# Two layered blocks on one core: the last norms moved behind their projections, modulation sums by transposes, and one projection reordered

## The reference, cut to what matters

```python
for layer in range(2):                         # first block
    shift, scale, gate = split(silu(c) @ ada_w[layer, 0] + ada_b[layer, 0])
    h = rms_norm(x, norm_w[layer, 0]) * (1.0 + scale) + shift
    y = hybrid_attention_mixer(h) if layer == 0 else multiscale_pool_mixer(h)
    x = x + gate * y
    shift, scale, gate = split(silu(c) @ ada_w[layer, 1] + ada_b[layer, 1])
    h = rms_norm(x, norm_w[layer, 1]) * (1.0 + scale) + shift
    x = x + gate * (square(relu(h @ w1[layer])) @ w2[layer])
x = rms_norm(x, final_norm_w)
# second block
x = x + concat(moba_attention, retention)(rmsnorm(x, attn_norm)) @ w_out
h = rmsnorm(x, ffn_norm)
u = causal_dwconv(h @ w_up, conv_w, conv_b)    # 3 taps along the tokens, each feature by itself
x = x + (gelu(u) * (h @ w_gate)) @ w_down      # inner width 2816
g = sigmoid(rmsnorm(x, ple_norm) @ w_ple_gate)
x = x + (p @ w_ple) * g
return rmsnorm(x, final_norm)
```

## Time and profile before

| | |
|---|---|
| median of 3 runs | 1028.75 us (1027.26 to 1029.9) |
| the profiled execution: its own time | 1026.28 us |
| its span | 1024.6 us |
| TensorE busy | 933.2 us, 91% |
| VectorE, ScalarE, GpSimd busy | 690.8, 446.6, 56.4 us |
| chain that ended last | TensorE 74%, VectorE 15%, waits for nothing shown 5%, ScalarE 4% |

### The profile page before, as it was taken

How to read it: one execution, slowest core, us unless ns; L and a number is a source line. 1 busy time by engine, 2 the same in 40 slices (tenths; PEclk the granted TensorE clock), 3 DMA queues, 4 the chain that set the end, 5 groups by cost and what they waited for, 6 DMA issues and landing times.

```text
span 1024.6 us, 17857 instructions
## 1 busy us (share of the span) xinstructions
PE 933.2 (91%) x7128; PEld 892.6 (87%) x7128; DVE 690.8 (67%) x877; ACT 446.6 (44%) x532; POOL 56.4 (6%) x102
## 2 busy tenths in 40 slices
PE   1599988999999999889999999999887999999976
PEld 1398865989999999779999999888787999999976
DVE  4757887678887777766655555865547776766457
ACT  2225533236664333356563334544533545443352
POOL 2101111021111000000000000000000000000000
PEclk9779975889999999699999999999998999999989
DMA  9829664439998787137665453734413655545511
GB/s 319 301 83 357 224 220 151 165 116 305 319 332 295 272 272 255 41 111 238 209 240 166 164 195 133 227 124 137 151 52 113 191 178 183 196 156 186 194 42 42
DMA packets 156457, 196.09 MB, mean 191 GB/s; under 512 B 5325, under 2 KB 143100, under 8 KB 156412
## 3 DMA queue, kind: packets, MB, share of 16 engines
q1 hardware_dynamic: 142588, 145.12, 44.0%
q0 software_dynamic: 13824, 50.34, 13.3%
HBM read 194.38 MB, written 1.06 MB: 191 GB/s over the span
## 4 chain that ended last, share of the span: by engine, by line
PE 74%; DVE 15%; issue 5%; ACT 4%; DMA 1%; SPq 1%; DVEq 0%; ACTq 0%; POOLq 0%
PE G L527 15%; PE G L528 14%; PE G L529 14%; PE A L527 7%; PE A L529 7%; PE A L528 7%; DVE w_lo L985 3%; ACT w_hi L1599 2%; PE A L631 1%; PE A L611 1%; DVE ada_acc L1003 1%; PE G L585 1%; DVE HN L1134 1%; PE G L587 1%; PE G L586 1%
## 5 line engine op out<-in xcount | busy, mean ns | idle before, releaser
L985 DVE TENSOR_TENSOR w_lo<-raw,w_hi 128x2048 fp32r<-128x2048 f32 (+1 forms) x135 | 307.2, 2275 | 217.3 <-ACT w_hi L1599 217.1
L527 PE MATMUL G<-h_hi,w_hi 128*128 128x256 f32 x1288 | 379.2, 294 | 29.3 <-DVE h_lo L1114 13.3
L1599 ACT ACTIVATE w_hi<-raw 128x2048 fp32r<-128x2048 f32 (+1 forms) x135 | 256.6, 1901 | 327.6 <-PE G L529 173.6
L528 PE MATMUL G<-h_lo,w_hi 128*128 128x256 f32 x1288 | 373.5, 290 | 0.0
L529 PE MATMUL G<-h_hi,w_lo 128*128 128x256 f32 x1288 | 372.9, 290 | 0.0
L527 PEld LDWEIGHTS G<-h_hi,w_hi 128*128 128x128 f32 x1288 | 256.3, 199 | 36.4 <-issue 24.5
L528 PEld LDWEIGHTS G<-h_lo,w_hi 128*128 128x128 f32 x1288 | 256.9, 199 | 0.8 <-issue 0.8
L529 PEld LDWEIGHTS G<-h_hi,w_lo 128*128 128x128 f32 x1288 | 256.6, 199 | 0.0
L527 PE MATMUL A<-u_hi,w_hi 128*128 128x256 f32 x512 | 144.2, 282 | 1.1 <-DVE X L1094 0.8
L528 PE MATMUL A<-u_lo,w_hi 128*128 128x256 f32 x512 | 143.5, 280 | 0.0
L529 PE MATMUL A<-u_hi,w_lo 128*128 128x256 f32 x512 | 143.5, 280 | 0.0
(11 more groups left out here) (279 smaller groups left out, 1092.8 us busy)
## 6 DMA issues: line engine op xcount, KB each, us to landing
raw<-in_mlp_w_dram SPq DMA_DIRECT2D x64, 1024.0 KB, 5.5
ada_raw<-in_ada_w_dram POOLq DMA_DIRECT2D x90, 512.0 KB, 5.3
raw<-in_w_in_dram SPq DMA_DIRECT2D x14, 1024.0 KB, 5.0
raw<-in_w_up_dram SPq DMA_DIRECT2D x11, 1024.0 KB, 5.2
raw<-in_w_gate_dram SPq DMA_DIRECT2D x11, 1024.0 KB, 5.3
raw<-in_attn_w_in_dram SPq DMA_DIRECT2D x9, 1024.0 KB, 12.1
raw<-in_w_down_dram SPq DMA_DIRECT2D x8, 1024.0 KB, 5.2
raw<-in_attn_w_out_dram SPq DMA_DIRECT2D x4, 1024.0 KB, 7.1
```

Of the source, the lines that this page charges most:

```text
L527: pe.matmul(dst, wh, ah, start=start, stop=False)
L528: pe.matmul(dst, wh, al, start=False, stop=False)
L985: dve.tensor_tensor(w_lo[n % 2][:, 0:k, :], raw[n % RAW][:, 0:k, :], w_hi[n % 2][:, 0:k, :].bitcast(F32), ALU.subtract).then_inc(lo_done, 1)
L1599: act.activation(w_hi[n % 2][:, 0:k, :], raw[n % RAW][:, 0:k, :], ACT.Copy).then_inc(hi_done, 1)
```

## The change

It has four parts.

- **Feed-forward and last gate on X times the norm weight.** While the second output projection runs, ScalarE and VectorE make `e_hi` and `e_lo` = X * weight after each residual, without rstd. Block 96 is an `early_block` with the mean square inside, and the other feed-forward blocks (`gated_block`) read `e_hi`, `e_lo`. `gated_up` on VectorE multiplies the bank by rstd into `UP`, in place of ScalarE's copy; the gate block is left without rstd, and `residual_tile` multiplies the down projection by it. The last gate's `h_hi`, `h_lo` are X * weight, made tile pair by tile pair in the down projection; its mean square comes after the second group of block 130; VectorE multiplies each gate bank by rstd into `HN`, and ScalarE takes the sigmoid of that.
- **Modulation sums by transposes** for layers 0, 1 and 3 (`turn_sums`, `part`): four transposes into a bank, two banks per part, and VectorE adds along the rows. Layer 2 keeps single-column matmuls (`add_sums`), a bank for each part.
- **First output projection**: each residual comes ahead of the next weights' rest and the `ada` steps; the last squares are made by ScalarE, and the mean square adds two sources, so it has four matmuls.
- **Order**: scale of layer 2, then its mean square, then shift (read by VectorE after the second `pad` tile) and gate; the sums of layer 3 come after the pooling block.

```diff
-                  ("flip1", 3), ("flip2", 0), ("flip3", 1), ("ms0", 2), ("mod0", 3), ("glr", 2))
+                  ("flip1", 3), ("flip2", 0), ("flip3", 1), ("ms0", 2), ("scale0a", 3), ("scale0b", 0), ("shift0a", 1),
+                  ("shift0b", 2), ("glr", 2))
...
-        take_each(("go0", 0), ("go1", 1), ("gm0", 2), ("gm1", 3), ("mod1", 3), ("ms1", 2), ("gate1", 3),
-                  ("mod2", 3), ("ms2", 2), ("gate2", 0), ("mod3", 1), ("gate3", 3), ("ms3", 2), ("ms4", 2), ("ms5", 3))
+        take_each(("go0", 0), ("go1", 1), ("gm0", 2), ("gm1", 3),
+                  ("scale1a", 3), ("scale1b", 0), ("shift1a", 1), ("shift1b", 3), ("ms1", 2), ("gate1a", 0),
+                  ("gate1b", 1), ("scale2", 3), ("ms2", 2), ("shift2", 3), ("gate2", 0), ("scale3a", 3),
+                  ("scale3b", 2), ("shift3a", 0), ("shift3b", 1), ("ms3", 3), ("gate3a", 2), ("gate3b", 3),
+                  ("ms4", 2), ("ms5", 3))
...
+            def turn_sums(m, name, blocks):
+
+                part = PARTS.index(name)
+                for half in range(2):
+                    dst = bank_empty(pe, f"{name}{m}{'ab'[half]}")
                     pe.wait_ge(ada_used, blocks)
+                    for t in range(4):
+                        at = (4 * half + t) * P
+                        last = pe.transpose(dst[:, t * P:(t + 1) * P], sums_of[m][:, part, at:at + P], ident)
+                    bank_done(f"{name}{m}{'ab'[half]}", last)
...
             scale_and_shift(1)
-            mean_square(1)
+            dst = bank_empty(pe, "ms1")
+            for k, squares in enumerate((sq_sum, sq)):
+                pe.wait_ge(ssq_ready, SQUARES[1] - 1 + k)
+                for m in range(2):
+                    last = pe.matmul(dst[:, 0:S], ones[:, :], squares[:, m, :], start=k + m == 0,
+                                     stop=k + m == 2)
+            bank_done("ms1", last)
             gate_sums(1)
             up(0)
             down(0)
-            scale_and_shift(2)
+            add_sums(2, "scale", 9 * DT)
             mean_square(2)
-            gate_sums(2)
-            scale_and_shift(3)
+            add_sums(2, "shift", 9 * DT)
+            add_sums(2, "gate", 9 * DT)
...
             last.then_inc(block_used, 1)
+            scale_and_shift(3)
             dst = bank_empty(pe, "ms3")
...
-            mean_square(6)
+            early_block(N_FFN, U_FFN, e6_ready, (1, 2, 3, 4), ((6,),))
+            gated_block(1)
             with pe.Fori(0, 5) as i:
-                for j in range(4):
-                    feature_block(N_FFN + j, U_FFN + j, i=i, split="n6" if j == 0 else None)
-            for j in (20, 21):
-                feature_block(N_FFN + j, U_FFN + j)
+                for j in range(2, 6):
+                    gated_block(j, i)
...
-                if g == 0:
+                if g == 1:
                     mean_square(7)
...
+                for half in "ab":
+                    src = bank_full(dve, f"{name}{m}{half}")
+                    t = 4 * "ab".index(half)
+                    ins = dve.tensor_reduce(part_sums[:, t:t + 4],
+                                            src[:, :].rearrange("p (t k) -> p t k", t=4), AX_X, ALU.add)
+                    bank_read(f"{name}{m}{half}", ins)
+                    bank_was_read(dve, f"{name}{m}{half}")
+                return dve.tensor_tensor(MOD[:, m, at:at + DT], part_sums[:, :], V[:, b:b + DT], ALU.add)
...
+            def modulation(m):
+
+                chain(part(m, "scale"))
+                factor(m)
+                part(m, "shift").then_inc(mod_ready, 1)
+                dve.wait_ge(mod_ready, m + (m < 2))
...
+                free = (down_free0, down_free1)[m]
                 if gate is None:
-                    ins = dve.tensor_tensor(xt, A[m][:, 0:S], xt, ALU.add)
+
+                    part = HN[0][:, m, :]
+                    dve.tensor_tensor(part, A[m][:, 0:S], rstd[:, :], ALU.mult).then_inc(free, 1)
+                    dve.wait_ge(free, 5 * phase + g + 2 + i)
+                    ins = dve.tensor_tensor(xt, part, xt, ALU.add)
...
-            for j in range(3):
-                split_lo(N_OUT + j + 2)
-                ada_next(1, (2, 1, 1)[j])
-                residual_pair(N_OUT + j, 9 + j, 2 * j, MOD[:, 0, 2 * DT:])
-            residual_pair(N_OUT + 3, 12, 6, MOD[:, 0, 2 * DT:])
+            for j in range(4):
+                residual_pair(N_OUT + j, 9 + j, 2 * j, MOD[:, 0, 2 * DT:], squares=j < 3)
+                if j < 3:
+                    split_lo(N_OUT + j + 2)
+                    ada_next(1, (2, 1, 1)[j])
...
+                if t == 1:
+                    part(2, "shift")
...
+            for j in range(4):
                 residual_pair(N_OUT2 + j, U_OUT2 + j, 2 * j, None)
-            residual_pair(N_OUT2 + 3, U_OUT2 + 3, 6, None)
-            norm("n6", 6, V[:, V_FFN2:V_FFN2 + DT])
+                if j < 3:
+                    split_lo(N_OUT2 + j + 2)
+                dve.wait_ge(e6_hi, j + 1)
+                for t in (2 * j, 2 * j + 1):
+                    ins = low_scaled(t, e_hi, e_lo, V[:, V_FFN2:V_FFN2 + DT])
+                ins.then_inc(e6_ready, 1)
...
             def gated_up(j, i=0):
 
                 u = U_FFN + j
+                dve.wait_ge(block_used, N_FFN + j + 1 + i * 4)
+                dve.tensor_tensor(UP[:, :, 2:], halves(G[u % 4]), spread(rstd[:, :], 2), ALU.mult
+                                  ).then_inc(g_free[u % 4], 1)
...
-                dve.wait_ge(g_free[u % 4], u // 4 + 1)
+                dve.wait_ge(block_used, N_PLEG + j + 1)
+                dve.tensor_tensor(HN[j % 2][:, :, :], halves(G[u % 4]), spread(rstd[:, :], 2), ALU.mult
+                                  ).then_inc(g_free[u % 4], 1)
+                dve.wait_ge(sg_ready, j + 1)
                 chain(dve.tensor_tensor(SG[:, :, :], SG[:, :, :], PE8[:, 2 * j:2 * j + 2, :], ALU.mult))
...
-            for j in range(4):
+            for j in range(3):
                 split_hi(N_OUT + j + 2)
+            act.wait_ge(g_free[0], 4)
+            act.wait_ge(ssq_ready, SQUARES[1] - 1)
+            act.activation(sq[:, :, :], X[:, 6:8, :], ACT.Square).then_inc(ssq_ready, 1)
+            split_hi(N_OUT + 5)
```

More of the change, by code:

```diff
@@ L1547, in _ @@
             chain.looped, chain.count = 0, start + 20
-            for j in (20, 21):
-                split_lo(N_FFN + j + 2)
-                (gated_gate if j % 2 else gated_up)(j)
             for g in range(4):
@@ L1558, in _ @@
                 split_lo(N_FDOWN + 3 * g + 4)
+                dve.wait_ge(hhi_ready, 4 * SPLIT["n7"] + g + 1)
+                for t in (2 * g, 2 * g + 1):
+                    ins = low_scaled(t, h_hi, h_lo, V[:, V_PLE2:V_PLE2 + DT])
+                ins.then_inc(h_ready, 1)
                 if g == 0:
```

156 lines of the change are left out of this document (88 added, 68 removed).

## The result

The changed kernel takes 1011.51 us (median of four runs, 1009.56 to 1014.23) against 1028.01 us for the kernel before beside it: a ratio of 0.9843, interval 0.9813 to 0.9873. Six more runs of it later gave 1013.33 us, a ratio of 0.9857 (0.9832 to 0.9883). All ten together have their median at 1012.9 us, and 80 runs of the kernel before theirs at 1027.1. The change gives 14.2 us where I forecast 8.6 (16.5 us in the first four runs, which fell low), and the first result lies 4.0 us under the lower end of my range. The sign was right, the size was not.

A forecast was written before the change was run, and what follows sets the result against it. TensorE was taken to bound the long weight-block stretches, leaving gains only between them. Terms 8.9 + 4.1 - 3.5 + 0.4 - 0.3 + 0.9 + 2.0 - 1.7 - 2.2 = 8.6 us gave 1017.7 us (1020.1 at the median), range 1015.5 to 1025.3.

The forecast's parts named there:

- So nothing is won inside a stretch.: Long weight-block stretches: TensorE is the bound at 0.120 us a matmul; only idle or half-clock time between stretches can be won.
- Feed-forward norm, 8.9: Start of the feed-forward: block 96 no longer waits for the norm, idle and half-clock time go; gain 8.9 us.
- Last norm 4.1: Norm before the last gate: TensorE's idle 6.01 us falls to 2.5 us, half-clock start stays; gain 4.1 us.
- tail 3.5: Last gate to end: VectorE waits for ScalarE's sigmoid, 1.38 us in series four times, and becomes the bound; loss 3.5 us.
- First projection, 2.0: First output projection and its norm: residuals ahead of `w_lo`, last squares on ScalarE, `HN` earlier; gain 2.0 us.
- Pooling, loss 3.9: Pooling layer: `shift2` and `ms3` each wait for bank 3, costing 1.7 and 2.2 us; loss 3.9 us.
- Layer 0, +0.4 and -0.3: Layer 0's modulation sums by transposes: scale and shift gain 0.4 us, gate 0 loses 0.3 us.
- gate 3, +0.9: Gate of layer 3: 16 TensorE passes become 8, VectorE's extra lies under weight blocks; gain 0.9 us.
- The clock falls in the sums: Rival: transposes also leave TensorE at 1.2 GHz, so `ms1` and `ms3` cost 5.2 us more: 1025.3 us; chance 0.12.
- Late start: Rival, first feed-forward blocks: VectorE and ScalarE arrive late, circle a little over 11.52 us; 3 us lost, 1023.1 us; chance 0.12.
- circle binds: Rival, `gated_up` in the feed-forward loop: circle through VectorE and ScalarE exceeds 11.52 us, slower than before, 1033 us; chance 0.04.
- More than I count: Rival: full clock at the last gate (2.0 us) and `shift2` at full clock (1.6 us): 1016.5 us; chance 0.15.

The follow-up runs named there:

- `e` and `h` at 192: Changed kernel with 64 bytes of unused tile ahead of `e_hi` and 64 more ahead of `gate_ps`: 1011.21 us, ratio 0.9846.
- `e` and `h` at 0: Changed kernel with 128 bytes of unused tile ahead of `e_hi` and 128 ahead of `gate_ps`: 1008.54 us, ratio 0.984.
- the free banks: Changed kernel with `shift2` and `ms3` in bank 1, last half of layer 3's shift sums behind its mean square: 1011.03 us, ratio 0.9844.
- the single runs: Kernel before with only the sums and order: 1028.0 us, ratio 1.0009; with only the reordered first output projection: 1028.88 us, 1.0014.
- the two pairs with like places: Old against changed kernel, `u` and `f` at 64 modulo 256: 1023.39 and 1012.9 us; `e`, `h`, `u`, `f` all at 64: 1006.08 and 1000.22 us.

## Why the forecast was wrong

- **"So nothing is won inside a stretch."** This is the step that failed. I read 0.120 us a matmul in the feed-forward and took it for the price of any weight block. The down projections ran at 0.117 already, which I did not look at, and the change moved them to 0.113 with a tile (`part_sums`) that my sum did not contain. Padding alone is worth 3.2 us on the old kernel and costs 4.4 when added to the new; that is most of the 5.6 us that I missed. The cause is shown from both sides: a pad alone brings the shorter pitch, and one pad too many takes it away. The two down projections have 1536 matmuls, and at 4 to 5 ns each that would be 6 to 8 us; in the profiles of the pad alone 2.5 and 0.6 us of it come out. Every fourth block of layer 0, at the turn of the loop, takes 6.1 to 6.3 us at either pitch, and layer 1 lost 1.7 us in that profile at the first up block, with more of it at half clock (a granted clock of 0.59 over the first 8.4 us, 0.81 in the kernel before).
- **Feed-forward norm, 8.9:** right. 8.3 us by the profiles' means (6.6 by the medians of that part alone, 3.9 to 8.5), block 96 without a wait, the mean square of 1.03 inside it. The loop stayed under TensorE: the product took 0.684 us for my 0.692 and VectorE's new 14 us cost nothing.
- **Last norm 4.1 and tail 3.5:** right in the profile. The last gate's first matmul starts 16.6 us earlier, 12.7 of it from the stages in front, so the norm gave 3.9; from there to the end it is 36.2 us for 32.6. The round trip is 1.38 as written, VectorE waits four times. Wrong was TensorE's last wait, 3.39 us and not over 5. Over all profiles the last column gained 1.7, for the kernels without this part scatter there by 1.9 us and the one I started from is in their shorter half. What I had named as a possible extra, full clock at the last gate (2.0 us), did come in three of the thirteen profiles with this part (`e` and `h` at 192, `e` and `h` at 0, the free banks): their last column is 39.7 and not 41.2, 1.5 us less. It came in no profile of the changed kernel itself. Busy time by stretch from the last gate's start, first with the free banks, then in the changed kernel:

```profile
969.10:975.90 6.80, 6.78 (x56) 6.80 (x57) 1.76 (x1) 2.08 (x4) 0.00 (x0) 1.00 0.01 2
```

```profile
971.80:978.60 6.80, 6.73 (x44) 6.76 (x45) 1.81 (x1) 1.43 (x3) 0.00 (x0) 0.75 0.00 0
```

- **First projection, 2.0:** right. Last weight matmul to root went from 7.3 to 5.4 us. Its working already had the short sums in it (207.15 to 208.9), but it stood under the projection's name, and before the single runs I gave the 2.0 to the order alone. Alone it is a loss of about 1.3 in that wait; it is a gain only with the short sums. A mean square behind the sums on one engine makes one term of two edits.
- **Pooling, loss 3.9:** right: 3.2 us by the means, and the waits of 1.58 and 2.25 stand where they were put (1.7 and 2.2). In the second profile of the changed kernel the first is 2.26. Another assignment of banks took the second away, and all but 1.0 of the first.
- **Layer 0, +0.4 and -0.3; gate 3, +0.9:** each is below what this kernel's profiles can tell; the reductions took 0.689 us for my 0.72.
- **The rivals.** None was this one. *The clock falls in the sums* did not happen at norm 1: in the changed kernel the stretch with 24 transposes and the mean square had full clock, and `ms1` took 1.90 us for eight passes:

```profile
203.90:208.60 4.70, 4.67 (x32) 4.04 (x32) 3.83 (x9) 3.25 (x4) 0.53 (x1) 1.00 0.99 310
```

  The Trainium skill ("TensorE: Matmul & The Clock Gate", "PE-mode transpose") says that the full clock does not engage for transposes; whether they could raise it, no row here shows, but in this stretch they did not lose it. *Late start* and *circle binds* did not happen either. *More than I count* had the right sign; of its two reasons the sums of layer 2 ran at half clock in every profile with the new order, and the full clock at the last gate was not there in the changed kernel's.

The account in us, against the 14.2 of the medians: forecast 8.6; places of `u` and `f` 3.2 to 4.4; last stage 1.1 more; pooling 0.7 more; feed-forward 0.6 less: 13.0 to 14.2. What is left is under what the runs can tell. The stage terms in it are means of single profiles, and by the two pairs with like places the 8.6 could as well be 6 or 10: the account adds up in part by luck.

## What to carry to other kernels

A new small tile can move large ones: before a change is credited with a time, look whether the untouched stages kept their pitch, and repeat the old kernel with a pad of the same size. Two edits around one in-order engine have to be priced together, for what stands behind the other's work decides. And where one profile scatters by 5 us in a stage, a sum made against a single execution needs that scatter in its range.

## What the runs showed of the hardware

At full granted clock and with the same instructions, matmuls of 128x256 (fp32r) start 113.3, 117 to 119, or 120 ns apart, and the place of the moving tile against the weight tile in a partition, modulo 256, goes with it. By kernel, moving tile's start less weight tile's: 0 gives 120 ns (all blocks on `h` and `e` before); 64 above gives 117.8; 128 gives 118.7 (5.70 us a block, in that kernel's up projections); 64 below gives 113.3 and in some stretches 117.8; 96 below 117.3 to 118.7; 32 below 118.3. The Trainium skill ("SBUF — State Buffer", "Who interferes with whom") says that TensorE waits on nobody there, its moving operand and its weight load having a read port each; these runs show that the two tiles' places matter all the same. Why 64 below has two levels, which change at block borders, from one stretch to the next and from one kernel to another with the same places, is open; so is whether it is the two reads that meet. No run moved the weight tiles alone, or the low parts against the high ones.
